# High and low parts of the 64 sample tokens side by side in one stationary block: two products in place of three

## The reference, cut to what matters

```python
def conv_mixer(h, hist, w_in, conv_w, conv_b, ln_g, ln_b, w_out):
    p = h @ w_in
    a, g_glu, z = jnp.split(p, 3, axis=-1)
    c = a * jax.nn.sigmoid(g_glu)
    ...
    y = jax.nn.silu(layernorm(y, ln_g, ln_b)) * jax.nn.silu(z)
    return y @ w_out, c_pad[:, -CONV_STATE:]

def sgu_mixer(h, chunk_len, w_in, ln_g, ln_b, w_s, s_bias, w_out):
    p = h @ w_in
    uv = jax.nn.gelu(p[..., :2 * E_B], approximate=False)
    z = p[..., 2 * E_B:]
    u, v = jnp.split(uv, 2, axis=-1)
    v = layernorm(v, ln_g, ln_b)
    ...
    s = (u5 * mixed).reshape(B, T, E_B) * jax.nn.silu(z)
    return s @ w_out, v
...
    xp = xp + rmsnorm(op, post_norm_g[i])
```

## Time and profile before

| | |
|---|---|
| median of 3 runs | 2299.09 us (2297.74 to 2300.61) |
| span of the profiled execution, first to last instruction | 2296.3 us |
| PE busy | 2260.8 us, 98% |
| DVE, ACT, POOL busy | 1581.8, 958.3, 365.3 us |
| mean granted clock of PE | 0.996 |

### The profile page before, as it was taken

One profiled execution on the slowest core, in us unless ns is written; L12 is line 12 of the kernel. 1 busy time (PEld: TensorE's weight loads), 2 busy tenths in 40 slices (PEclk: granted clock), 3 DMA queues, 4 the chain that ended last, 5 costly groups with the idle time before them and its releaser, 6 DMA issues.

```text
span 2296.3 us, 30420 instructions
## 1 busy us (share of the span) xinstructions
PE 2260.8 (98%) x12074; PEld 1971.1 (86%) x12074; DVE 1581.8 (69%) x1947; ACT 958.3 (42%) x1429; POOL 365.3 (16%) x519
## 2 busy tenths in 40 slices
PE   8899999999999999999999999999999999999998
PEld 7788899999887887888887888877789999998886
DVE  5599988997597988999985237742286666666221
ACT  6333333333353215665664125531135655565110
POOL 3111111111221101211110101211012121210000
PEclk9999999999999999999999999999999999999999
DMA  4346566656444412333335425342213333336330
GB/s 171 115 129 160 160 157 182 166 140 166 138 148 167 139 61 93 116 120 121 100 119 218 159 90 211 138 165 84 80 63 92 94 100 100 95 95 249 111 100 28
DMA packets 131838, 295.11 MB, mean 129 GB/s; under 512 B 17777, under 2 KB 54385, under 8 KB 130162
## 3 DMA queue, kind: packets, MB, share of 16 engines
q1 hardware_dynamic: 102674, 194.35, 25.4%
q0 software_dynamic: 29024, 98.83, 15.3%
HBM read 214.75 MB, written 78.75 MB: 128 GB/s over the span
## 4 chain that ended last, share of the span: by engine, by line
PE 94%; DMA 2%; DVE 2%; ACT 1%; issue 1%; POOL 0%; SPq 0%; DVEq 0%; ACTq 0%
PE PS L2111 30%; PE PS L2112 30%; PE PS L2113 30%; PE PS L2332 2%; PE PS L2202 1%; PE PS L2180 1%; DMA yb<-y_scratch 1%; DMA raw<-wa_in_in 1%; PE PS L2122 1%; DMA st<-s_scratch 0%; PE PS L2189 0%; DVE xn L1527 0%; DMA rawb<-wb_out_in 0%; PE PS L2335 0%; DVE S4r L1875 0%
## 5 line engine op out<-in xcount | busy, mean ns | idle before, releaser
L1559 DVE SCALAR_TENSOR_TENSOR acc<-cp,cw,acc 128x513 f32<-128x513 f32 (+3 forms) x464 | 367.9, 793 | 14.2
L2111 PE MATMUL PS<-HAh,Wh 128*128 128x512 f32 (+3 forms) x968 | 343.0, 354 | 0.2 <-DVE HAl L1517 0.2
L2112 PE MATMUL PS<-HAl,Wh 128*128 128x512 f32 (+3 forms) x968 | 341.0, 352 | 0.0
L2113 PE MATMUL PS<-HAh,Wl 128*128 128x512 f32 (+3 forms) x968 | 340.9, 352 | 0.0
L2111 PE MATMUL PS<-Wbh,s7h 128*128 128x512 f32 (+1 forms) x544 | 214.2, 394 | 6.8 <-DVE Wbl L1517 5.2
L2111 PE MATMUL PS<-Vh,HBh 128*128 128x512 f32 (+1 forms) x544 | 212.5, 391 | 2.5 <-DVE Vl L1517 2.5
L2112 PE MATMUL PS<-Wbl,s7h 128*128 128x512 f32 (+1 forms) x544 | 212.9, 391 | 0.0
L2113 PE MATMUL PS<-Wbh,s7l 128*128 128x512 f32 (+1 forms) x544 | 212.8, 391 | 0.0
L2112 PE MATMUL PS<-Vl,HBh 128*128 128x512 f32 (+1 forms) x544 | 211.9, 390 | 0.0
L2113 PE MATMUL PS<-Vh,HBl 128*128 128x512 f32 (+1 forms) x544 | 211.9, 389 | 0.0
L2111 PEld LDWEIGHTS PS<-HAh,Wh 128*128 128x128 f32 x968 | 182.5, 189 | 15.1 <-DVE HAl L1517 0.4
(11 more groups left out here) (217 smaller groups left out, 5195.5 us busy)
## 6 DMA issues: line engine op xcount, KB each, us to landing
raw<-wa_in_in SPq DMA_DIRECT2D x48, 512.0 KB, 4.0
Wl<-wa_in_in POOLq DMA_DIRECT2D x39, 512.0 KB, 5.5
rawv<-wb_v_in SPq DMA_DIRECT2D x64, 256.0 KB, 4.6
QWr<-wb_uz_in SPq DMA_DIRECT2D x64, 256.0 KB, 2.6
v_scratch<-vb POOLq DMA_DIRECT2D x64, 256.0 KB, 2.6
vt<-v_scratch SPq DMA_DIRECT2D x32, 512.0 KB, 3.9
s_scratch<-m POOLq DMA_DIRECT2D x32, 512.0 KB, 4.1
rawb<-wb_out_in SPq DMA_DIRECT2D x28, 512.0 KB, 7.6
```

The costliest lines, as they stand in the source:

```text
L1559: return nc.vector.scalar_tensor_tensor(out=out, in0=src, scalar=w, in1=first, op0=ALU.mult, op1=ALU.add)
L2111: nc.tensor.matmul(out, wh, xh, start=start, stop=False, skip_group_check=seeded)
L2112: nc.tensor.matmul(out, wh, xl, start=False, stop=False, skip_group_check=seeded)
L2113: return nc.tensor.matmul(out, wl, xh, start=False, stop=stop, skip_group_check=seeded)
```

## The change

For tile 16 (named `TAIL`) the 64 high columns and the 64 low columns stand side by side in one stationary block of 128 columns. `pair` multiplies it by the high part of the weights and then by the low part, into one bank. Partitions 0 to 63 then hold high times (high + low), and 64 to 127 hold low times (high + low); this has the product low times low as well. ACT copies partitions 64 to 127 out to a buffer on partitions 0 to 63, and DVE adds them to partitions 0 to 63 (`tail_sum`) before anything else reads the bank. In O and B the low part is written into the free right half of the high part's buffer. In V a new buffer, `HBpair`, gets a second copy of both parts; the old ones are still made, as Q reads them. POOL's `rsqrt` is rewritten to count on one shared semaphore, with the same instructions.

The diff, cut to its core: the two helpers; for O the pieces of ACT's `o_square`, DVE's `v_stage` and PE's `o_product`; for V those of ACT's `n2_high` and `v_stage` and DVE's `n2_low`; for B those of ACT's `b_end_squares` and DVE's `b_gain`. PE's products of V and B, and DVE's sum in V, are changed as in O.

```diff
+            def pair(out, x, wh, wl, start, stop):
+                nc.tensor.matmul(out, x, wh, start=start, stop=False)
+                return nc.tensor.matmul(out, x, wl, start=False, stop=stop)
...
+            def tail_sum(out, low, count):
+                dve.wait_ge(t_copy, count)
+                nc.vector.tensor_tensor(out, out, low, ALU.add).then_inc(t_sum, 1)
...
+                if t == TAIL:
+                    nc.scalar.activation(ob[h].xn[s][0:n, :], banks(2 * s)[low_half(t), :], ACT.Copy).then_inc(t_copy, 1)
+                    act.wait_ge(t_sum, 1)
                 square_mean(ob[h].xn[s][0:n, :], banks(2 * s)[0:n, :], ss3[0:n, s:s + 1], o_sq)
...
+                if last == TAIL:
+                    m = rows(last)
+                    tail_sum(banks(2 * (last % 2))[0:m, :], ob[h].xn[last % 2][0:m, :], 1)
                 v_low(h, 0, 3)
                 o_gain(last)
...
+                if t == TAIL:
+                    return pair(PS[:, 2 * s + c, :], o.sh[s][:, k, :], Woh[:, k, 512 * c:512 * (c + 1)],
+                                Wol[:, k, 512 * c:512 * (c + 1)], k == 0, k == KD - 1)
...
+                if t == TAIL:
+                    nc.scalar.activation(HBpair[:, :, 0:rows(t)], src, ACT.Copy)
...
+                        if first + i == TAIL:
+                            nc.scalar.activation(vb[u % 5][0:m, :], PS[low_half(TAIL), v_bank(h, q, i), :], ACT.Copy)\
+                                .then_inc(t_copy, 1)
+                            act.wait_ge(t_sum, q + 2)
                         nc.scalar.activation(vb[u % 5][0:m, :], PS[0:m, v_bank(h, q, i), :], ACT.Gelu).then_inc(v_gel, 1)
...
+                if t == TAIL:
+                    nc.vector.tensor_tensor(HBpair[:, :, low_half(t)], src, in_half(HBh[h], t).bitcast(fp32), ALU.subtract)
...
                 act.wait_ge(o_main, bi(t) + 2)
+                nc.scalar.activation(t7b[0:n, 512:D], PS[low_half(t), b + 1, :], ACT.Copy).then_inc(t_copy, 1)
+                act.wait_ge(t_sum, NQ + 3)
                 square_mean(t7b[0:n, 512:D], PS[0:n, b + 1, :], ss_end[0:n, :], o_sq)
...
+                if t == TAIL:
+                    for c in range(2):
+                        tail_sum(PS[0:n, b_pair(t) + c, :], t7b[0:n, 512 * c:512 * (c + 1)], NQ + 2 + c)
```

More of the change, by code:

```diff
@@ L319, in build @@
         gu = [gu0, at(r1_at + 26112, "gu1", [P, WIDTH[1]])]
+        HBpair = at(e_at, "HBpair", [P, KD, P], f32r)
         t7b = at(r2_at + 65536, "t7b", [P, D])
@@ L602, in s7_next, with low_half @@
             return [TILES[h][k]] if k < len(TILES[h]) and (h, i) != (0, 3) else []
+        TAIL = NTILES - 1
+        def low_half(t):
+            return slice(rows(t), 2 * rows(t))
         def b_pair(t):
@@ L918, in _, with add_eps, rsqrt @@
         def _(pool):
-            def rsqrt(src, dst, n, added, done, count):
-                nc.gpsimd.tensor_scalar(src[0:n], src[0:n], EPS, None, ALU.add).then_inc(added, 1)
-                pool.wait_ge(added, count)
+            eps_sums = [0]
+            def add_eps(src):
+                nc.gpsimd.tensor_scalar(src, src, EPS, None, ALU.add).then_inc(p_eps, 1)
+                eps_sums[0] += 1
+                pool.wait_ge(p_eps, eps_sums[0])
+            def rsqrt(src, dst, n, done):
+                add_eps(src[0:n])
                 nc.gpsimd.tensor_tensor(dst[0:n], src[0:n], half_neg[0:n, 0:1], ALU.pow).then_inc(done, 1)
@@ L937, in n1_rsqrt @@
                 s = slice(t, t + 1)
-                rsqrt(ss1[:, s], rn1[:, s], rows(t), n1_eps, n1_r, t + 1)
+                rsqrt(ss1[:, s], rn1[:, s], rows(t), n1_r)
             def c_store(b):
@@ L966, in ln_rsqrt @@
                 pool.wait_ge(o_agg, t + 1)
-                rsqrt(mv[:, t % 2, 1:2], rs3[:, t % 2:t % 2 + 1], rows(t), o_eps, o_rs, t + 1)
+                rsqrt(mv[:, t % 2, 1:2], rs3[:, t % 2:t % 2 + 1], rows(t), o_rs)
             def o_step(h, i):
@@ L973, in o_step @@
                     pool.wait_ge(o_sq, oi(t) + 1)
-                    rsqrt(ss3[:, t % 2:t % 2 + 1], r23[:, t % 2:t % 2 + 1], rows(t), o_eps2, o_r2, oi(t) + 1)
+                    rsqrt(ss3[:, t % 2:t % 2 + 1], r23[:, t % 2:t % 2 + 1], rows(t), o_r2)
                 if 0 <= i + 2 < n:
@@ L979, in o_step @@
                     pool.wait_ge(n2_sq, t + 1)
-                    rsqrt(ss2[:, t % 2:t % 2 + 1], rn2[:, t % 2:t % 2 + 1], rows(t), n2_eps, n2_r, t + 1)
+                    rsqrt(ss2[:, t % 2:t % 2 + 1], rn2[:, t % 2:t % 2 + 1], rows(t), n2_r)
                     nc.gpsimd.dma_start(rows_of(x1_d, t), ob[h].x1[t % 2][0:rows(t), :]).then_inc(o_st[t % 2], 16)
@@ L1057, in b_stage @@
                         continue
-                    rsqrt(ss7[:, t % 2:t % 2 + 1], r27[:, t % 2:t % 2 + 1], rows(t), o_eps2, o_r2, bi(t) + 1)
+                    rsqrt(ss7[:, t % 2:t % 2 + 1], r27[:, t % 2:t % 2 + 1], rows(t), o_r2)
                     pool.wait_ge(o_post, bi(t) + 1)
@@ L1676, in o_low @@
                 dve.wait_ge(o_sh, t + 1)
[L1677 removed]
+                low = o.sh[s][:, :, low_half(t)] if t == TAIL else o.sl[s][:, :, 0:n]
+                split_low(low, o.zb[s][:, :, 0:n], o.sh[s][:, :, 0:n], o_sl)
             def n2_low(t):
@@ L2286, in v_product @@
                 s, n = (NQ * h + q) % 2, rows(t)
+                if t == TAIL:
+                    return pair(PS[:, v_bank(h, q, i), :], HBpair[:, k, :], Vh[s][:, k, :],
+                                Vl[s][:, k, :], k == 0, k == KD - 1)
                 return three(PS[0:n, v_bank(h, q, i), :], in_half(HBh[h], t)[:, k, :], in_half(HBl[h], t)[:, k, :],
```

39 lines of the change are left out of this document (23 added, 16 removed).

## The result

The changed kernel took 2286.46 us (median of 5 runs, 2284.61 to 2287.84), beside 2299.09 us for the kernel before on the same chip (5 runs, 2297.3 to 2300.61). The ratio is 0.9945 [0.9934, 0.9956]: 12.6 us faster, where 14.8 were forecast.

A forecast was written before the change was run, and what follows sets the result against it. PE, busy 98% of the span, was taken as the bound. V 7.57 - 1.35, B 7.57 - 1.35 and O 2.37 gave 14.81 us: 2299.1 - 14.8 = 2284.3 us, own range 2282 to 2287, wider range 2280.5 to 2288.5.

The forecast's parts named there:

- The spacing: Tile 16 in O, V, B: 128-column matmuls at 226.7 ns, old ones at 230.0; 18.93 us saved if nothing waits.
- The 55 ns of a wider load: Rival: each of the 160 products up to 55 ns dearer, 8.8 us in all, time 2293.1 us; chance 0.06.
- the slower rival: Load of 128 columns not pulled ahead of the matmul, 415 ns for two products, time 2314.4 us; chance 0.03.
- The sums: Copy and sum of 512 columns delay what follows by 1.35 us; covered in V's first three quarters, not at V to Q.
- The end: B, second half: copy and sum stand between PE's last matmul and the last squares; loss 1.35 us.
- O to V: Of O's 3.79 us only 2.37 arrive; V's first weights are late on DVE, PE stands 1.6 us.
- The clock at V to Q: Rival: a pause, grown from 1.00 to about 2.4 us at V to Q, halves PE's clock; 3.0 us, 2287.3; chance 0.10.
- the shorter kind: Reason against a clock fall: new pause resembles the 2.46 us one with no fall, not the 2.55 us one with a fall.
- if the granted clock falls behind one of the longer pauses: One of the signs by which the prediction would be wrong, to be seen in the profile after.
- that fall at 2090 doesn't occur: Part of the rival that less is lost (chance 0.11): no clock fall at 2090 us, +3.0 us, about 2281.3 us.
- The prediction's best case: Less is lost: O to V gives its full 3.79 (+1.4), no clock fall at 2090 (+3.0); 2280.9 us; chance 0.11.
- The offset: Profiled execution taken to be a run like the timed ones, whose median is 2.79 us above its span.

The follow-up runs named there:

- e8: Changed kernel with the pairs' stationary block cut to its 64 high columns, sample tokens' low part left out: 2286.7 us, one execution.
- e4: Changed kernel keeping all copies and sums, but with three products of 64 tokens as before: 2301.4 us, 1.0011 to the kernel before.
- e7: Changed kernel with V's first low part made ahead of tile 15's scaling on DVE in half 1: 2283.87 us, 0.993 to the kernel before.
- V alone: Changed kernel with the change kept in stage V only, O and B with three products: 2294.15 us, 0.9978 to the kernel before.
- e12: Changed kernel with ACT's `copy_ab` in half 1 moved behind S3's second high part and S1's: 2290.35 us, 0.9958 to the kernel before.
- e9: Changed kernel run again with no edit: 2288.8 us, 0.9945 to the kernel before.
- e10: Changed kernel with V's first low part ahead of tile 15's scaling and `copy_ab` ahead of S3's high part: 2282.65 us, 0.9926 to the kernel before.
- e11: Kernel before with V's first low part ahead of tile 15's scaling and `copy_ab` ahead of S3's high part: 2299.53 us, 0.9996.

## Why the prediction was right, point by point

**The spacing, right.** 226.7 ns for the pairs, 7.57 us in B. The 55 ns of a wider load don't show, as e8 settles with its narrow loads. With that the slower rival falls too.

**The sums, right.** 1.35 us from copy to what follows, at V to Q and at the end, and hidden elsewhere, by e4. The end measured +1.24 where 1.35 were put. Copy to squares is the full 1.35 there; of the 0.1 us between, 0.06 is that DVE's `b_gain` starts 0.72 us behind the second squares in place of 0.78 (2276.86 behind 2276.14, before 2290.32 behind 2289.54), and the rest lies in steps of up to 0.04 ahead of the copy and behind the store's issue.

**O to V, right.** V began 9.74 us behind tile 16's first matmul, as worked out. The pause was put at 1.6, counted from the end of the last matmul's spacing; counted so it measured 1507.65 - 1505.83 - 0.23 = 1.59 us (the profile's 1.44 takes the modelled end of that matmul). The reason given (DVE's queue) is shown by e7, which brought back 1.20 of the 1.42 us.

**The clock at V to Q, a rival that came true in part.** The forecast assumed that PE keeps its clock behind a pause of about 2.4 us, and called 3.0 us the price if not. The pause came as said (2.36). Behind a pause of 2.35 or 2.36 at this place the clock fell in three profiles of six (the change, V alone, where the fall began 0.2 us before PE resumed, and 64 columns) and not in the other three (the sums alone, e7, the change again). Where it fell, it was for 3.41 us, at a price of 1.4 to 1.6 us: 1.54 here, half of what the rival was given. All fourteen profiles, kernel before included, give these counts:

| place | pause, us | clock fell in |
|---|---|---|
| V to Q, half 1 | 0.56 to 1.00 | 0 of 7 |
| O to V, half 1 | up to 1.44 | 0 of 14 |
| V to Q, half 1 | 2.35, 2.36 | 3 of 6 |
| O to V, half 0, same instructions up to there in all | 2.45, 2.46 | 7 of 14 |
| V to Q, half 1 (e12) | 4.80 | 1 of 1 |
| B's start, half 1 | 2.55 to 4.57 | 13 of 14 |

The fourth line is the pause from which the prediction took its reason against the rival: "a pause of 2.46 us with no fall behind it", and so the new pause was "the shorter kind". In e7, at the same place and with the same pause, the clock fell (PE's timeline and windows):

```profile
702.24 0.79 PE L2158 MATMUL PS<-Vh,HBh 128*128 128x512 f32 x1 [2.46 <-DVE Vl L1544]
```

```profile
703.00:705.00 2.00, 2.00 (x7) 0.50 1.00 362
```

The trace of before itself holds a fall behind a shorter pause, 1.61 us in O of half 0, where PE waited for a transfer:

```profile
614.82 0.66 PE L2180 MATMUL PS<-con,yb 128*128 128x128 f32 x4 [1.61 <-DMA yb<-y_scratch]
```

```profile
616.00:619.00 3.00, 3.00 (x9) 0.53 0.53 178
```

So one trace did not carry that reason, and a chance of 0.10 was too low. One of the prediction's own signs of being wrong, "if the granted clock falls behind one of the longer pauses", came true in the profile after: on this point it was wrong. That the forecast held all the same is in part luck, since the fall costs half of what was put. This, the missing +1.54, is most of the difference between the 13.5 us of the spans and the forecast 14.8; the other stretches add up to -0.2.

**The rival "that fall at 2090 doesn't occur", wrong by its size.** It was given +3.0 us. In e9 there was no fall at B's start, and B up to tile 16 took 178.23 us, as it did in the change with 3.41 us of half clock, beside 178.44 before with 6.83. In all fourteen profiles this stretch took 178.23 to 178.61 us, so a fall costs between nothing and 0.4 us there. The prediction's best case is also added up wrongly: with 1.4 and 3.0 us less than 2284.3 it is 2279.9, not 2280.9. PE's timeline shows why the fall costs so little, first in e9, at full clock:

```profile
2083.37 0.50 PE L2155 MATMUL PS<-Wbh,s7h 128*128 128x512 f32 x1 [3.35 <-DVE Wbl L1544]
...
2086.06 0.50 PE L2155 MATMUL PS<-Wbh,s7h 128*128 128x512 f32 x1 [1.04 <-DVE Wbl L1544]
```

and in the change, whose clock had fallen (granted 0.69 from 2081 to 2085 us):

```profile
2084.54 0.79 PE L2155 MATMUL PS<-Wbh,s7h 128*128 128x512 f32 x1 [0.29 <-DVE Wbl L1544]
```

The second block of B starts 2086.06 - 2083.37 = 2.69 us behind the first in e9, and 2084.54 - 2081.85 = 2.69 us in the change. The weights set the pace; half clock only fills what was idle time.

**The offset, wrong, and without effect.** The median of before was compared with the span of its profiled execution, 2.79 us apart. In every execution with both numbers the time is 1.8 us above the span (1.7 to 1.9), so the profiled one of before was about 2298.1, some 1.0 us below its median. The forecast was made from the median and needed no offset to be 14.8 below it. The profiled execution of the change lies 1.85 us below its median. That is why the medians differ by 12.6 us where the spans differ by 13.5: the 0.9 us between lie within the scatter of the runs (3 us from least to most in either kernel).

**Open.** B's first weights came later in kernels with two products in V: PE's pause at B's start was 2.9 to 4.6 us, beside 2.55 to 2.69 in those without. The pause hangs on a transfer: in before, the change, e9 and e10 B's first product starts 2.39 or 2.40 us behind the landing of the first of its raw weights. In before and in e9 SP issued that transfer 368.34 us behind Q's second product, and from issue to landing it took (start and duration in the chain that ended last; before first, then e9):

```profile
2079.35 7.07 DMA rawb<-wb_out_in
```

```profile
2073.09 7.88 DMA rawb<-wb_out_in
```

So it landed 0.81 us later, and PE's pause is 0.80 longer. In the change it was the issue that came later (370.78 us, of which the fall of the clock explains 1.54), with a landing in 6.51 us; in e10 both did (369.49 and 8.61). Why is not settled; no experiment changed the traffic or the moment of the issue. Why 64 stationary columns cost 3.3 ns more than 128 is not settled either.

## What to carry to other kernels

Price a matmul by the spacing of starts in rows of its own form: where products of half a tile cost as much as those of a full one, filling the other half with the low part and dropping one product in three is gain, less the copy and sum that join the halves. These cost only where a queue ends a stage; look there at what stands ahead of the instruction that PE waits for. A shorter stream can make an order worth more than it was (2.64 us at the two places in e10, 0.75 in e11), but follow the gain to the next stage: between e9 and e10 1.9 of the 2.64 us were lost again at the next waits. And a pause that grows from 1.0 to 2.35 us, as here, can cost the clock behind it besides its own length; one trace in which it didn't fall is no proof that it won't.

## What the runs showed of the hardware that was not expected

- A pause of 2.35 us at V to Q was followed by a fall of the clock in three profiles of six, and in one of two of the changed kernel itself; one of 2.46 us at O to V of half 0 in seven of fourteen, with the same instructions ahead of it in all. In e9 PE stood for 3.35 us at B's start, and from 2082 to 2096 us the granted clock was 1.00 all the same. A single profile can't tell whether a change brings the fall.
- The first stretch, up to tile 16 of O in half 1, has the same instructions in all fourteen profiles, and took 1497.91 to 1498.93 us in seven of them and 1499.54 to 1501.65 in the others. The first group had 6.83 us of half clock in the first 100 us, the second about 10.2. The means are 1.9 us apart, and 1.5 us of it is there already at PE's 501st matmul, some 113 us in: a part of the runs' scatter is decided in the first 100 us, and an edit elsewhere is better read from its own stretch than from the time.
- 512 columns against 64 stationary columns are spaced 230.0 ns, against 128 columns 226.7, although the load is 134 ns for the one and 188 for the other.
